# Encoder trunk on one core: the expert choice, ranks and slot lists made tile by tile inside the output projection, with four buffers of gathered rows

## Chip, cores and metric

One core of a Trainium2 chip runs the whole kernel in one launch. The metric is the device time of one execution in microseconds (us); lower is better.

## Reference

The reference is a trunk of two layers over 512 tokens of 1024 features, in float32. Layer 0 mixes tokens by windowed attention, layer 1 by a bidirectional gated DeltaNet. Both end with an output projection added to x, a row norm, and the same mixture of experts, cut here to what matters:

```python
def hierarchical_moe(h, w_group, b_group, w_expert, b_expert, w_gate, w_up, w_down):
    g_logits = t @ w_group + b_group                       # 4 groups
    g_prob, g_idx = lax.top_k(softmax(g_logits), 1)        # the best group
    e_sel = (t @ w_expert + b_expert).reshape(-1, 4, 8)[g_idx]
    e_prob, e_idx = lax.top_k(softmax(e_sel), 2)           # two of its 8 experts
    gate = g_prob * e_prob / sum(e_prob)
    hid = silu(t @ w_gate[e]) * (t @ w_up[e])              # 32 experts, 1024 -> 256
    return sum over the two experts of gate * (hid @ w_down[e])
```

## The kernel before

Tokens lie in four tiles (TT) of 128 rows. The order of the work is written out by hand for each engine, and semaphores join the engines. No planner is involved.

**Output projection** (`project_back_pe`, line 313). Two halves of 512 output columns, four tiles in each. One block is eight steps c of three matmuls (`three`, lines 142 to 144). In the second half each finished tile goes through a chain: VectorE adds the block to x (370), ScalarE squares the rows (249), VectorE and GpSimd make the root (263, 254), VectorE writes the normed rows hn (266), GpSimd stores them to h_rows in HBM (825), TensorE turns them (276), ScalarE and VectorE copy the two halves of the turned rows (288, 302), and TensorE multiplies them with the router (`route_pe`, 353: eight matmuls of 36 columns). VectorE adds the bias (359). `turn_routed` and `route_pe` for one tile stand behind the projection block of a later tile. The text calls the second half's block of tile t "block t"; route and turn of tile t are "route t" and "turn t".

**Choice and lists.** When all four tiles have logits, `moe_dve` (line 1046) works on all four at once: three times the first maximum (`first_max`: best group, best expert, second expert), one-hot rows `oh`, and their sum `oh_sum` (1074). TensorE counts with triangular and all-ones matrices (931 to 938) the rank of each token in its expert. VectorE picks the ranks (1084, 1086), compares them with slot numbers (1090), and eight matmuls of line 942 make the list of tokens of each expert. VectorE turns that into indices `idx_i` (1096).

**Experts.** GpSimd gathers the 64 slots of an expert from h_rows by an indirect DMA (`gather`, 833) into one of AHEAD = 8 row buffers, and scatters results to y_rows (`scatter`, 840). Its loop is

```python
for e in range(AHEAD):
    gather(e)
for e in range(EXPERTS):
    scatter(e)                      # waits y_copied of e
    if e + AHEAD < EXPERTS:
        gather(e + AHEAD)
```

TensorE runs for each expert e: gate and up (957), turn of the rows of e+1 (949), down of e-1 (966), turn of the hidden rows (999). VectorE copies the result of down (1119).

**Weights.** SyncE loads them in order (`moe_sync`, 2082): two of 1 MB for gate and up (2068) and one of 1 MB for down (2074) per expert. There are six homes for gate and up and five for down. Experts 1 and 2 may load when the first half of the projection is done, 3 when the second is, 4 when route 3 is (its home is ht), 5 when the normed rows are stored (its home is hn). From expert 6 on, gate and up wait until TensorE has used the home, and down of expert 5 waits for down of expert 0.

Of the kernel before, what the change touches and what calls it, by code (L numbers as in the profile page):

```python
# [10 lines left out]
AX = mybir.AxisListType.X  # L11

P = 128
D = 1024
# [25 lines left out]
AHEAD = 8  # L40
# [4 lines left out]
def build(nc, ap, out):  # L45
    ctx = ExitStack()
    with ctx:
# [265 lines left out]
        def project_back_pe(pe, k, n, tpk):  # L313
            for half in range(2):
                for t in range(TT):
# [383 lines left out]
        def masks_dve(dve, o):  # L699
# [15 lines left out]
            for l in range(1, LEVELS):  # L715
# [12 lines left out]
        at_xgt = ml.at  # L728
        xgt = ml.take(RING, KC * SLOTS)
        gated = ml.take(F // 2)  # L730
        at_hidden = ml.at
        hidden = ml.take(RING, F // 2)
        hidden_t = ml.take(RING, 2 * SLOTS)
        at_y = ml.at
# [34 lines left out]
        PER = dict(most=1, stored=16 * TT, routed=TT, logits=TT, pool_c=1, dve=2, exp_g=1, exp_e=1, onehots=1,  # L769
                   ranks=1, pos=1, placed=2 * TT, lists=1, idx=1, combined=TT)  # L770
# [156 lines left out]
        def moe_pe(pe, l):  # L927
            pe.wait_ge(s["onehots"], 1 + l * PER["onehots"])

            pe.matmul(bank[1][:, 0:TT * EXPERTS], upper[:, :], oh_sum.rearrange("p t e -> p (t e)"),  # L930
                      start=True, stop=False)
            for k in range(TT - 1):
                pe.matmul(bank[1][:, (k + 1) * EXPERTS:TT * EXPERTS].rearrange("p (t e) -> p t e", e=EXPERTS),
                          ones[:, :], oh_sum[:, k:k + 1, :].to_broadcast([P, TT - 1 - k, EXPERTS]),
                          start=False, stop=k == TT - 2)
            for k in range(TT):
                last = pe.matmul(bank[1][:, TT * EXPERTS:(TT + 1) * EXPERTS], ones[:, :], oh_sum[:, k, :],
                                 start=k == 0, stop=k == TT - 1)
            last.then_inc(s["ranks"], 1)
            for n in range(2 * TT):  # L940
                pe.wait_ge(s["placed"], n + 1 + l * PER["placed"])
                last = pe.matmul(bank[2][:, 0:2 * EXPERTS], at_slot[:, n // TT, n % TT, :],
                                 entries[:, n // TT, n % TT, :], start=n == 0, stop=n == 2 * TT - 1)
            last.then_inc(s["lists"], 1)

# [99 lines left out]

        def moe_dve(dve, l, o):
            lg = logits[:, :, 0:GROUPS]

# [3 lines left out]
            def first_max(src, n, col, dst):  # L1052

                o.step(dve.tensor_reduce(stat[:, col, :], src, AX, ALU.max))
                kk = key[:, :, 0:n]
                o.step(dve.tensor_tensor(kk, src, bc(stat[:, col, :], n), ALU.is_equal))
                o.step(dve.tensor_tensor(kk, kk, revs[:, 0:n].unsqueeze(1).to_broadcast([P, TT, n]), ALU.mult))
                o.step(dve.tensor_reduce(stat[:, 15, :], kk, AX, ALU.max))
                o.step(dve.tensor_tensor(dst, kk, bc(stat[:, 15, :], n), ALU.is_equal))

            dve.wait_ge(s["pool_c"], 1 + l * PER["pool_c"])
            dve.wait_ge(s["logits"], TT * (l + 1))
            first_max(lg, GROUPS, 0, oh_g)
            dve.tensor_tensor(g_exp, lg, bc(stat[:, 0, :], GROUPS), ALU.subtract).then_inc(s["dve"], 1)
            o.step(dve.tensor_scalar(oh_g, oh_g, -1.0, -REPEL, ALU.add, ALU.mult))
            e4 = "p t (g e) -> p t g e"
            o.step(dve.tensor_tensor(masked[:, 0].rearrange(e4, g=GROUPS),
                                     logits[:, :, GROUPS:].rearrange(e4, g=GROUPS),
                                     oh_g.unsqueeze(3).to_broadcast([P, TT, GROUPS, PER_GROUP]), ALU.add))
# [1242 lines left out]
```

## Time and profile before

| | |
|---|---|
| median of three runs | 1407.58 us (1407.0 to 1412.06) |
| the profiled execution, its own time | 1407.08 us |
| its span, first to last instruction | 1405.5 us |
| TensorE busy | 1223.2 us, 87% |
| VectorE / ScalarE / GpSimd busy | 584.0 / 384.5 / 464.5 us |
| mean granted TensorE clock | 0.945 |
| DMA | 270.29 MB, mean 192 GB/s |

The profile is one execution. "Busy" is the sum of the instructions of an engine. A float32 matmul shows as two records. The chain of waits follows the last instruction back to what released it; "issue" in it is time with nothing to see behind it. A window gives busy time, granted clock and the mean busy share of the 16 DMA engines. "To landing" is the time from the issue of a DMA to its completion.

### The profile page before, as it was taken

How to read it: one execution, taken by the hardware profiler on the slowest of the kernel's cores; microseconds unless marked ns; L12 is line 12 of the kernel's file. 1: busy time of each engine (PE TensorE's matmuls, PEld its weight loads, DVE VectorE, ACT ScalarE, POOL GpSimd, SP SyncE). 2: the span in 40 equal slices, each digit the busy share in tenths (PEclk: the TensorE clock that was granted, in tenths of full speed). 3: DMA queues.
4: the chain of work that ended last, by engine and by line, in shares of the span. 5: the costliest groups of instructions: out<-in, count | busy, mean ns of one | idle time of the engine just before them, and what ended most of it. 6: DMA issues, size and time to landing. Idle time of an engine off the chain costs nothing. (4 is left out here: it accounts for less than half of the span.)

```text
span 1405.5 us, 19363 instructions
## 1 busy us (share of the span) xinstructions
PE 1223.2 (87%) x7621; PEld 903.8 (64%) x7621; DVE 584.0 (42%) x1197; ACT 384.5 (27%) x804; POOL 464.5 (33%) x468
## 2 busy tenths in 40 slices
PE   5989999879998885889788999888999789998783
PEld 4867677755555552778677887678888755544451
DVE  4456754421111114564686455776464421111113
ACT  4325651111100012363433354433442211110000
POOL 1221001122222211046778247877221132222110
PEclk9999999879999998899999999999999889999997
DMA  7122004669999997211000111000235679999996
GB/s 219 61 66 76 1 1 187 249 255 374 382 388 388 385 409 316 80 60 60 2 0 1 60 61 60 1 0 2 97 113 211 267 282 377 395 386 378 386 417 238
DMA packets 65803, 270.29 MB, mean 192 GB/s; under 512 B 16812, under 2 KB 16908, under 8 KB 41136
## 3 DMA queue, kind: packets, MB, share of 16 engines
q1 hardware_dynamic: 54176, 247.50, 46.3%
q0 software_dynamic: 11392, 21.00, 4.5%
q8 instruction: 63, 1.03, 0.3%
q10 hardware_dynamic: 144, 0.52, 0.1%
q14 instruction: 28, 0.23, 0.1%
HBM read 262.69 MB, written 23.07 MB: 203 GB/s over the span
## 5 line engine op out<-in xcount | busy, mean ns | idle before, releaser
L840 POOL DMA_INDIRECT y_rows<-arena,idx_i x64 | 64.4, 1006 | 370.8 <-DVE arena L1119 362.6
L1455 PE MATMUL bank<-arena 128*128 128x128 f32 x1088 | 141.3, 287 | 16.8 <-DVE arena L1974 7.4
L1455 PEld LDWEIGHTS bank<-arena 128*128 128x128 f32 x1088 | 132.2, 199 | 29.4 <-DVE arena L1974 11.6
L957 PE MATMUL bank<-ring,arena 128*64 128x256 f32 x1024 | 127.8, 402 | 20.8 <-issue 19.8
L1123 DVE TENSOR_TENSOR arena<-arena,bank 128x128 f32<-128x128 f32 x64 | 18.4, 288 | 287.7 <-ACT arena L1034 287.7
L1034 ACT ACTIVATE arena<-bank 128x128 f32<-128x128 f32 x64 | 17.8, 277 | 388.3 <-PE bank L957 388.3
L957 PEld LDWEIGHTS bank<-ring,arena 128*64 128x64 f32 x1024 | 78.2, 139 | 60.0 <-issue 24.2
L144 PE MATMUL bank<-ring_r,ht_r 128*128 128x512 f32 x288 | 114.0, 396 | 0.0
L1119 DVE COPY arena<-bank 128x512 f32<-128x512 f32 x64 | 44.3, 692 | 144.4 <-PE bank L966 144.4
L142 PE MATMUL bank<-ring_r,arena_r 128*128 128x512 f32 (+1 forms) x228 | 92.2, 404 | 6.3 <-DVE ring_r L166 3.4
L143 PE MATMUL bank<-ring_r,arena_r 128*128 128x512 f32 x224 | 89.0, 398 | 0.0
L949 PEld LDWEIGHTS bank<-ident,arena 64*128 64x128 f32 x512 | 61.3, 200 | 34.9 <-issue 25.1
L143 PE MATMUL bank<-ht_r,ring_r 128*128 128x512 f32 (+1 forms) x224 | 82.0, 366 | 0.0
L833 POOL DMA_INDIRECT arena<-h_rows,idx_i x64 | 60.9, 952 | 61.6 <-DVE idx_i L1096 42.7
L949 PE MATMUL bank<-ident,arena 64*128 64x64 f32 x512 | 70.1, 278 | 9.4 <-DMA arena<-h_rows,idx_i 9.4
L1859 DVE SCALAR_TENSOR_TENSOR arena<-bank,arena 128x511 f32<-128x511 f32 (+1 forms) x72 | 54.0, 750 | 52.2 <-ACT arena L1572 50.5
L966 PE MATMUL bank<-ring,arena 128*64 128x512 f32 x304 | 73.6, 605 | 1.5 <-DVE arena L1128 1.5
L1782 POOL TENSOR_TENSOR arena<-ring,arena 128x512 f32<-128x512 f32 x48 | 61.9, 1309 | 6.9 <-PE bank L1455 6.9
L1757 POOL TENSOR_SCALAR arena<-arena,move 128x512 f32<-128x512 f32 x40 | 63.0, 1585 | 2.1 <-PE bank L1460 2.1
L144 PEld LDWEIGHTS bank<-ring_r,ht_r 128*128 128x128 f32 x288 | 55.2, 192 | 11.9
L276 PE MATMUL bank<-ident,hn 128*128 128x128 f32 x192 | 31.7, 320 | 33.3 <-DVE hn L266 31.5
L142 PE MATMUL bank<-ring_r 128*128 128x512 f32 (+1 forms) x144 | 56.8, 395 | 4.2 <-DVE ht_r L296 2.2
(297 smaller groups left out, 2373.7 us busy)
## 6 DMA issues: line engine op xcount, KB each, us to landing
ring<-in_moe_w_down SPq DMA_DIRECT2D x38, 1024.0 KB, 27.8
ring<-in_moe_w_gate SPq DMA_DIRECT2D x32, 1024.0 KB, 25.3
ring<-in_moe_w_up SPq DMA_DIRECT2D x32, 1024.0 KB, 27.8
ring<-in_gdn_w_in SPq DMA_DIRECT2D x8, 2048.0 KB, 8.2
arena<-in_moe_w_down SPq DMA_DIRECT2D x14, 1024.0 KB, 28.2
arena<-in_moe_w_gate SPq DMA_DIRECT2D x12, 1024.0 KB, 24.7
arena<-in_moe_w_up SPq DMA_DIRECT2D x12, 1024.0 KB, 26.6
gain<-in_moe_w_down SPq DMA_DIRECT2D x12, 1024.0 KB, 28.4
```

Source lines behind the costliest of these rows:

```text
L142: pe.matmul(dst, a[0], b[0], start=start, stop=False)
L143: pe.matmul(dst, a[0], b[1], start=False, stop=False)
L144: return pe.matmul(dst, a[1], b[0], start=False, stop=stop)
L833: pool.indirect_dma_start(out=rows_of(e), out_offset=None, in_=h_rows[l], in_offset=bass.IndirectOffsetOnAxis(ap=idx_i[0:SLOTS, 0, e:e + 1 ...
L840: pool.indirect_dma_start(out=y_rows[l], out_offset=bass.IndirectOffsetOnAxis(ap=idx_i[:, 1, e:e + 1], axis=0), in_=y_out[:, e % RING, :], ...
L949: last = pe.transpose(bank[0][:, c * SLOTS:(c + 1) * SLOTS], rows_of(e)[:, c::KC], ident[at, at])
L957: last = pe.matmul(bank[1][m * SLOTS:(m + 1) * SLOTS, 0:2 * P].rearrange("p (w n) -> p w n", w=2), xgt[:, i, c * SLOTS:(c + 1) * SLOTS], w ...
L966: last = pe.matmul(bank[3][half * SLOTS:(half + 1) * SLOTS, :], hidden_t[:, i, m * SLOTS:(m + 1) * SLOTS], d[:, m, half * HALF:(half + 1) ...
L1455: last = pe.matmul(bank[b][:, h * P:(h + 1) * P], lhs(h), rhs(h), start=True, stop=True)
L1757: pool.tensor_scalar(s_buf[slot], r_buf[l % 2][slot], move[:, l:l + 1], None, ALU.mult).then_inc(g["rb"], 1)
L1782: pool.tensor_tensor(lm[slot], lt_of(n), by_head(level[l]), ALU.mult).then_inc(g["lm"], 1)
L1859: last = dve.scalar_tensor_tensor(out=acc, in0=bank[U % 4][:, of], scalar=tap(k, unit), in1=acc, op0=ALU.mult, op1=ALU.add)
```

## The change

The choice moves from `moe_dve` into the projection. VectorE runs route_dve and `choose_dve` of tile 0 ahead of its wait for block 2, and of tile 1 ahead of block 3; tiles 2 and 3 follow behind the projection. Route 0 and route 1 on TensorE stand now inside blocks 2 and 3, behind their step c = 1. Ranks are made per tile from a running sum (`oh_upto`), lists per tile, and the totals last, behind the list. Scratch of the choice moves to where row buffers 4 to 7 were, so AHEAD is 4: four gathers are issued ahead, and gather e+4 stands behind scatter e. `first_max` has four operations on one tile where it had five on all four.

```diff
 RING = 3
-AHEAD = 8
+AHEAD = 4
...
                             split_done(pe, n + half, c)
                         last = three(pe, bank[u % 4][:, :], ht_parts(tpk, c, slice(t * P, (t + 1) * P)),
                                      panel_parts(n + half, c, slice(0, PANEL)), c == 0, c == KC - 1)
+                        if half and t >= 2 and c == 1:
+                            route_pe(pe, k, tpk + 1, t - 2)
                     last.then_inc(back, 1)
                     if k and u == 0:
                         pe.wait_ge(g["ready"], TT)
@@ -330,12 +332,42 @@
                     if half and t:
                         pe.wait_ge(ln["rows"], TT * (2 * k + 1) + t)
                         turn_routed(pe, k, tpk + 1, t - 1)
-                    if half and t >= 2:
-                        route_pe(pe, k, tpk + 1, t - 2)
             route_pe(pe, k, tpk + 1, TT - 2)
             pe.wait_ge(ln["rows"], TT * (2 * k + 1) + TT)
             turn_routed(pe, k, tpk + 1, TT - 1)
+            for t in range(2):
+                ranks_pe(pe, k, t)
             route_pe(pe, k, tpk + 1, TT - 1)
+            ranks_pe(pe, k, 2)
+            for t in range(2):
+                lists_pe(pe, k, t)
+            ranks_pe(pe, k, 3)
+            for t in range(2, TT):
+                lists_pe(pe, k, t)
+
+        def rank_bank(t):
+            return bank[(1, 1, 3, 0)[t]][:, t * EXPERTS:(t + 1) * EXPERTS]
+
+        def ranks_pe(pe, l, t):
+            if t == 0:
+                pe.wait_ge(x_half, 2 * TT * l + 2 * TT)
+            pe.wait_ge(s["onehots"], TT * l + t + 1)
+            at = rank_bank(t)
+            last = pe.matmul(at, upper[:, :], oh_sum[:, t, :], start=True, stop=t == 0)
+            if t:
+                last = pe.matmul(at, ones[:, :], oh_upto[:, t - 1, :], start=False, stop=True)
+            last.then_inc(s["ranks"], 1)
+
+        def lists_pe(pe, l, t):
+            for k in range(2):
+                pe.wait_ge(s["placed"], 2 * TT * l + 2 * t + k + 1)
+                last = pe.matmul(bank[2][:, 0:2 * EXPERTS], at_slot[:, k, t, :], entries[:, k, t, :],
+                                 start=t + k == 0, stop=t + k == TT)
+            if t == TT - 1:
+                last.then_inc(s["lists"], 1)
+                pe.wait_ge(s["totals"], l + 1)
+                pe.matmul(bank[3][:, 0:EXPERTS], ones[:, :], oh_upto[:, TT - 1, :], start=True, stop=True
+                          ).then_inc(s["counted"], 1)
 
         def turn_routed(pe, l, k, t):
...
 
         x_half = sem("x_half")
 
-        def project_back_dve(dve, k, tpk):
+        def project_back_dve(dve, k, tpk, o):
             for half in range(2):
                 for t in range(TT):
                     u = TT * half + t
+                    if half and t >= 2:
+                        route_dve(dve, k, t - 2)
+                        choose_dve(dve, k, t - 2, o)
                     dve.wait_ge(back, 2 * TT * k + u + 1)
                     dst = x[:, t, half * PANEL:(half + 1) * PANEL]
                     dve.tensor_tensor(dst, dst, bank[u % 4][:, :], ALU.add).then_inc(x_half, 1)
@@ -372,11 +407,14 @@
                         if t:
                             turn_dve(dve, tpk + 1, t - 1)
                         norm_dve(dve, 2 * k + 1, t)
-                        if t >= 2:
-                            route_dve(dve, k, t - 2)
             route_dve(dve, k, TT - 2)
+            groups_dve(dve, k, TT - 2, o)
             turn_dve(dve, tpk + 1, TT - 1)
+            experts_dve(dve, k, TT - 2, o)
+            for t in range(2):
+                place_dve(dve, k, t, o)
             route_dve(dve, k, TT - 1)
+            choose_dve(dve, k, TT - 1, o)
 
         def project_back_act(act, k, tpk):
...
-        at_slot = cut(at_xgt, 2, TT, P)
-        entries = cut(at_y, 2, TT, 2 * EXPERTS)
-        key = cut(at_hidden, TT, EXPERTS)
-        oh_sum = cut(at_hidden + TT * EXPERTS, TT, EXPERTS)
-        masked = cut(at_hidden + 2 * TT * EXPERTS, 2, TT, EXPERTS)
+        rl = Layout()
+        rl.at = AHEAD // 2 * D
+        at_slot = rl.take(2, TT, P)
+        at_entries = rl.at
+        entries = rl.take(2, TT, 2 * EXPERTS)
+        key = rl.take(EXPERTS)
+        masked = rl.take(2, EXPERTS)
+        placed_in = rl.take(2, EXPERTS)
+        oh_sum = rl.take(TT, EXPERTS)
+        oh_upto = rl.take(TT, EXPERTS)
+        assert rl.at <= 2 * D * 2
+        pos_parts = cut(at_entries, 2, TT, EXPERTS)
...
         def moe_pe(pe, l):
-            pe.wait_ge(s["onehots"], 1 + l * PER["onehots"])
...
-            last.then_inc(s["lists"], 1)
...
 
+        def first_max(dve, o, src, n, t, col, dst, op, scale):
+
+            o.step(dve.tensor_reduce(stat[:, col, t:t + 1], src, AX, ALU.max))
+            kk = key[:, 0:n]
+            o.step(dve.scalar_tensor_tensor(out=kk, in0=src, scalar=stat[:, col, t:t + 1], in1=revs[:, 0:n],
+                                            op0=ALU.is_equal, op1=ALU.mult))
+            o.step(dve.tensor_reduce(stat[:, 15, t:t + 1], kk, AX, ALU.max))
+            o.step(dve.tensor_scalar(dst, kk, stat[:, 15, t:t + 1], scale, op, ALU.mult))
+
+        def groups_dve(dve, l, t, o):
+            if t == 0:
+                dve.wait_ge(s["pool_c"], 1 + l * PER["pool_c"])
+            dve.wait_ge(s["logits"], TT * l + t + 1)
+            first_max(dve, o, logits[:, t, 0:GROUPS], GROUPS, t, 0, oh_g[:, t, :], ALU.is_lt, REPEL)
+            e4 = "p (g e) -> p g e"
+            o.step(dve.tensor_tensor(masked[:, 0].rearrange(e4, g=GROUPS), logits[:, t, GROUPS:].rearrange(e4, g=GROUPS),
+                                     oh_g[:, t, :].unsqueeze(2).to_broadcast([P, GROUPS, PER_GROUP]), ALU.add))
+
+        def experts_dve(dve, l, t, o):
+            first_max(dve, o, masked[:, 0], EXPERTS, t, 1, oh[:, 0, t, :], ALU.is_equal, 1.0)
+            o.step(dve.scalar_tensor_tensor(out=masked[:, 1], in0=oh[:, 0, t, :], scalar=2 * REPEL, in1=masked[:, 0],
+                                            op0=ALU.mult, op1=ALU.add))
+            first_max(dve, o, masked[:, 1], EXPERTS, t, 2, oh[:, 1, t, :], ALU.is_equal, 1.0)
+            last = dve.tensor_tensor(oh_sum[:, t, :], oh[:, 0, t, :], oh[:, 1, t, :], ALU.add)
+            if t < TT - 1:
+                o.step(last)
+                last = dve.tensor_scalar(oh_upto[:, t, :], oh_sum[:, t, :], 0.0, None, ALU.add) if t == 0 else                     dve.tensor_tensor(oh_upto[:, t, :], oh_upto[:, t - 1, :], oh_sum[:, t, :], ALU.add)
+            last.then_inc(s["onehots"], 1)
+            for k in range(2):
+                dve.tensor_tensor(entries[:, k, t].rearrange("p (w e) -> p w e", w=2),
+                                  oh[:, k, t].unsqueeze(1).to_broadcast([P, 2, EXPERTS]),
+                                  listed[:, k, :, t].unsqueeze(2).to_broadcast([P, 2, EXPERTS]), ALU.mult)
+
+        def choose_dve(dve, l, t, o):
+            groups_dve(dve, l, t, o)
+            experts_dve(dve, l, t, o)
+
+        def place_dve(dve, l, t, o):
+            dve.wait_ge(s["ranks"], TT * l + max(t + 1, 2))
+            found = rank_bank(t)
+            o.step(dve.tensor_tensor(placed_in, oh[:, :, t, :], found.unsqueeze(1).to_broadcast([P, 2, EXPERTS]),
+                                     ALU.mult))
+            o.step(dve.tensor_reduce(rank_f[:, :, t], placed_in, AX, ALU.add))
+            for k in range(2):
+                dve.tensor_scalar(at_slot[:, k, t, :], slot_no, rank_f[:, k, t:t + 1], None, ALU.is_equal
+                                  ).then_inc(s["placed"], 1)
+
         def moe_dve(dve, l, o):
...
+            dve.tensor_tensor(g_exp, logits[:, :, 0:GROUPS], bc(stat[:, 0, :], GROUPS), ALU.subtract
+                              ).then_inc(s["dve"], 1)
             dve.tensor_tensor(stat[:, 5, :], stat[:, 2, :], stat[:, 1, :], ALU.subtract).then_inc(s["dve"], 1)
...
+            for t in range(2, TT):
+                place_dve(dve, l, t, o)
+            dve.wait_ge(s["onehots"], TT * (l + 1))
+            dve.tensor_tensor(oh_upto[:, TT - 1, :], oh_upto[:, TT - 2, :], oh_sum[:, TT - 1, :], ALU.add
+                              ).then_inc(s["totals"], 1)
             dve.wait_ge(s["lists"], 1 + l * PER["lists"])
             for w in range(2):
                 last = dve.tensor_scalar(idx_i[:, w, :], bank[2][:, w * EXPERTS:(w + 1) * EXPERTS],
                                          first_of[:, w:w + 1], None, ALU.add)
             last.then_inc(s["idx"], 1)
+            dve.wait_ge(s["counted"], 1 + l * PER["counted"])
+            o.step(dve.tensor_reduce(most_f, bank[3][:, 0:EXPERTS], AX, ALU.max))
+            dve.tensor_copy(most_i[:, :], most_f).then_inc(s["most"], 1)
             for k in range(2):
-                last = dve.tensor_tensor(masked[:, k], oh[:, k], base.unsqueeze(1).to_broadcast([P, TT, EXPERTS]),
...
```

## Rows read from the trace of the kernel before

**Rows 1.** Windows of layer 1: length, busy us (instructions) by engine, clock, DMA share, GB/s.

```profile
1130.00:1135.00 5.00, 1.37 (x10) 1.22 (x12) 0.90 (x6) 0.94 (x2) 3.78 (x5) 0.50 0.52 153
1210.00:1220.00 10.00, 10.00 (x72) 5.21 (x70) 2.06 (x5) 0.86 (x2) 2.41 (x3) 1.00 1.03 395
1260.00:1270.00 10.00, 7.32 (x52) 4.29 (x50) 1.40 (x4) 0.86 (x2) 1.96 (x2) 1.00 1.02 361
```

**Rows 2.** Chain of waits, layer 1, late experts: start, us, what.

```profile
1260.33 2.67 issue
```

**Rows 3.** Timeline, layer 1, second half of the projection: start us, us, engine, line.

```profile
1090.43 0.48 PE L142 MATMUL bank<-ring_r,arena_r 128*128 128x512 f32 x1
...
1104.14 1.04 PE L276 MATMUL bank<-ident,hn 128*128 128x128 f32 x8
...
1104.34 0.69 DVE L370 TENSOR_TENSOR x<-x,bank 128x512 f32<-128x512 f32 x1 [4.01 <-PE bank L144]
...
1105.01 3.69 PE L353 MATMUL bank<-router,ht 128*128 128x36 f32 x32
...
1106.11 0.56 ACT L288 COPY ht<-bank 128x512 f32<-128x512 f32 x1
...
1107.07 1.28 DVE L266 SCALAR_TENSOR_TENSOR hn<-x,norm_s,gain 128x1024 f32<-128x1024 f32 x1 [0.68 <-POOL norm_s L254]
...
1110.57 3.28 PE L353 MATMUL bank<-router,ht 128*128 128x36 f32 x16 [0.88 <-DVE ht L302]
```

**Rows 4.** Timeline, layer 1, choice, lists, first gather and turn.

```profile
1114.19 0.17 DVE L1054 TENSOR_REDUCE arena<-arena 128x4 f32<-128x16 f32 x1
...
1114.39 0.18 DVE L1056 TENSOR_TENSOR arena<-arena 128x16 f32<-128x16 f32 x1
...
1119.41 0.29 DVE L1074 TENSOR_TENSOR arena<-arena 128x128 f32<-128x128 f32 x1
...
1121.48 1.89 PE L937 MATMUL bank<-arena,ones 128*128 128x32 f32 x8
...
1124.39 1.66 DVE L1090 TENSOR_SCALAR arena<-arena 128x128 f32<-128x128 f32 x8
...
1124.74 3.68 PE L942 MATMUL bank<-arena 128*128 128x64 f32 x16 [1.36 <-DVE arena L1090]
...
1129.74 1.04 POOL L833 DMA_INDIRECT arena<-h_rows,idx_i  x1 [20.52 <-DVE idx_i L1096]
...
1132.81 1.14 PE L949 MATMUL bank<-ident,arena 64*128 64x64 f32 x8 [4.39 <-DMA arena<-h_rows,idx_i]
```

**Rows 5.** Timeline, layer 1, loop over experts: turns of 3 and 4, gather of 5.

```profile
1152.70 1.09 PE L949 MATMUL bank<-ident,arena 64*128 64x64 f32 x8
...
1158.53 0.95 POOL L833 DMA_INDIRECT arena<-h_rows,idx_i  x1 [0.30 <-issue]
...
1159.63 1.09 PE L949 MATMUL bank<-ident,arena 64*128 64x64 f32 x8
```

**Rows 6.** Timeline, layer 0: last add, first gather and turn.

```profile
264.19 0.69 DVE L370 TENSOR_TENSOR x<-x,bank 128x512 f32<-128x512 f32 x1 [4.02 <-PE bank L144]
...
291.26 1.04 POOL L833 DMA_INDIRECT arena<-h_rows,idx_i  x1 [22.17 <-DVE idx_i L1096]
...
294.89 1.15 PE L949 MATMUL bank<-ident,arena 64*128 64x64 f32 x8 [5.01 <-DMA arena<-h_rows,idx_i]
```

**Rows 7.** DMA issues between 1116 and 1118 us: KB, us to landing.

```profile
gain<-in_moe_w_down SPq DMA_DIRECT2D x1, 1024.0 KB, 15.0
```

**Rows 8.** DMA issues between 1129.5 and 1130 us, the first gather.

```profile
arena<-h_rows,idx_i POOLq DMA_INDIRECT x1, 3.0
```

**Rows 9.** DMA issues between 1151 and 1152 us, the gather of expert 4.

```profile
arena<-h_rows,idx_i POOLq DMA_INDIRECT x1, 6.9
```

**Rows 10.** All gathers: us to landing.

```profile
DMA to landing us min/median/max: 2.8/7.6/8.9
```

**Rows 11.** DMA queues of the whole span: packets, MB, share of 16 engines.

```profile
q0 software_dynamic: 11392, 21.00, 4.5%
```

More of the change, by code:

```diff
@@ L768, in build @@
         late_step = [sem(f"late_step{l}") for l in range(2)]
-        PER = dict(most=1, stored=16 * TT, routed=TT, logits=TT, pool_c=1, dve=2, exp_g=1, exp_e=1, onehots=1,
-                   ranks=1, pos=1, placed=2 * TT, lists=1, idx=1, combined=TT)
+        PER = dict(most=1, totals=1, counted=1, stored=16 * TT, routed=TT, logits=TT, pool_c=1, dve=2, exp_g=1, exp_e=1, onehots=TT,
+                   ranks=TT, pos=1, placed=2 * TT, lists=1, idx=1, combined=TT)
         PER.update({n: EXPERTS for n in ("st", "turned", "xgt", "up", "silu", "hidden", "hid_turned", "hid_t",
@@ L927, in moe_pe @@
         def moe_pe(pe, l):
-            pe.wait_ge(s["onehots"], 1 + l * PER["onehots"])
[L930 to L943, printed above, removed]
-            last.then_inc(s["lists"], 1)
             def turn_rows(e):
@@ L1046, in moe_dve @@
         def moe_dve(dve, l, o):
-            lg = logits[:, :, 0:GROUPS]
             def bc(v, n):
                 return v.unsqueeze(2).to_broadcast([P, TT, n])
[L1052 to L1069, printed above, removed]
@@ L1070, in moe_dve @@
-            first_max(masked[:, 0], EXPERTS, 1, oh[:, 0])
-            o.step(dve.scalar_tensor_tensor(out=masked[:, 1], in0=oh[:, 0], scalar=2 * REPEL, in1=masked[:, 0],
-                                            op0=ALU.mult, op1=ALU.add))
-            first_max(masked[:, 1], EXPERTS, 2, oh[:, 1])
-            dve.tensor_tensor(oh_sum, oh[:, 0], oh[:, 1], ALU.add).then_inc(s["onehots"], 1)
-            dve.tensor_tensor(stat[:, 5, :], stat[:, 2, :], stat[:, 1, :], ALU.subtract).then_inc(s["dve"], 1)
@@ L1076, in moe_dve @@
-            for k in range(2):
-                dve.tensor_tensor(entries[:, k].rearrange("p t (w e) -> p t w e", w=2),
-                                  oh[:, k].unsqueeze(2).to_broadcast([P, TT, 2, EXPERTS]),
-                                  listed[:, k].rearrange("p w t -> p t w").unsqueeze(3).to_broadcast(
-                                      [P, TT, 2, EXPERTS]), ALU.mult)
-            dve.wait_ge(s["ranks"], 1 + l * PER["ranks"])
-            found = bank[1][:, 0:TT * EXPERTS].rearrange("p (t n) -> p t n", t=TT)
@@ L1083, in moe_dve @@
-            for k in range(2):
-                last = dve.tensor_tensor(masked[:, k], found, oh[:, k], ALU.mult)
-            o.step(last)
-            o.step(dve.tensor_reduce(rank_f.rearrange("p k t -> p (k t)"), masked.rearrange("p k t e -> p (k t) e"),
-                                     AX, ALU.add))
-            for k in range(2):
-                for t in range(TT):
-                    dve.tensor_scalar(at_slot[:, k, t, :], slot_no, rank_f[:, k, t:t + 1], None, ALU.is_equal
-                                      ).then_inc(s["placed"], 1)
@@ L1098, in moe_dve @@
             last.then_inc(s["idx"], 1)
+            dve.wait_ge(s["counted"], 1 + l * PER["counted"])
+            o.step(dve.tensor_reduce(most_f, bank[3][:, 0:EXPERTS], AX, ALU.max))
+            dve.tensor_copy(most_i[:, :], most_f).then_inc(s["most"], 1)
             for k in range(2):
-                last = dve.tensor_tensor(masked[:, k], oh[:, k], base.unsqueeze(1).to_broadcast([P, TT, EXPERTS]),
+                last = dve.tensor_tensor(pos_parts[:, k], oh[:, k], base.unsqueeze(1).to_broadcast([P, TT, EXPERTS]),
                                          ALU.mult)
             o.step(last)
-            o.step(dve.tensor_reduce(pos_f.rearrange("p k t -> p (k t)"), masked.rearrange("p k t e -> p (k t) e"),
-                                     AX, ALU.add))
+            o.step(dve.tensor_reduce(pos_f.rearrange("p k t -> p (k t)"),
+                                     pos_parts.rearrange("p k t e -> p (k t) e"), AX, ALU.add))
             o.step(dve.tensor_tensor(pos_f, pos_f, rank_f, ALU.add))
@@ L2288, in _ @@
             gdn_dve(dve, o)
-            project_back_dve(dve, 1, 4)
+            project_back_dve(dve, 1, 4, o)
             moe_dve(dve, 1, o)
```

8 lines of the change are left out of this document (2 added, 6 removed).

## The prediction

> **What bounds the kernel now.** I read the windows first, then the chain of waits, the timeline around the end of the projection, and last the DMA issues. From 1210 us on, a window of layer 1 has the DMA engines at a share of 1.03 and 395 GB/s while TensorE is fully busy; from 1260 us the share is still 1.02, but TensorE is busy for 7.32 of 10 us [rows 1], and the chain shows why: 2.67 us of "issue" ahead of a gate and up, which is a wait for weights [rows 2]. An expert needs 3 x 1024 KB = 3.15 MB, at 395 GB/s 7.96 us. TensorE needs only 1159.63 - 1152.70 = 6.93 us for an expert [rows 5]. So the stage of the experts is bound by the weight stream, after TensorE has first run through what was prefetched. The one hole in the stream is at its start: at 1130 to 1135 us the DMA share is 0.52 [rows 1], because all homes are full and nothing is freed until the first experts are done. The end of each layer therefore stands at a fixed distance behind the moment when expert 0 is turned and multiplied, and this moment is what the change can shift. Two layers, two shifts; everything behind a layer moves along with it.
>
> From the last add of x (E, 1104.34) to the first gather is 25.4 us in layer 1 [rows 3, 4], 27.1 us in layer 0 (264.19 to 291.26) [rows 6]. This stretch holds small work in single file, and is what the change shortens.
>
> **1. Inside blocks 2 and 3.** From the start of block 2 to E are 13.9 us [rows 3], and they contain two blocks, one turn and route 0. Now they contain route 1 too. 16 route records at full clock are 3.69/2 = 1.85 us [rows 3]. At step c = 1 TensorE has to wait for the copies of the turned tile: the ScalarE copy ends 1106.11 + 0.56 - 1104.34 = 2.33 us behind an add [rows 3], which itself starts some 0.1 behind the block, against 2.3 us of turn and six matmuls. With a wake-up that is about 0.2 us a block, taken as 0.35 for both. E moves by **+2.2 us**. VectorE's choice of a tile lies beside this. It has five operations for the group, nine for the experts, two for the sums, two for the entries: 18. Small operations follow each other by 1114.39 - 1114.19 = 0.20 us [rows 4], with 32 columns I take 0.22, so 3.9 us. It can start when the route inside the block ends, and 18 matmuls at 0.23 us (5.5 us for a block's 24) are 4.1 us more of the block. It just fits; if this cover is gone, each us too many delays the add behind it, and at tile 3 E itself.
>
> The Trainium skill, page "VectorE: DVE Perf Modes", section "The TRN2 errata — SBUF-src ops pay a fixed extra latency per instruction", speaks against this part: many small tiles pay a fixed cost per tile that one large one pays once. The trace agrees: 0.17 us for 16 columns, 0.29 us for 128 [rows 4], so four tiles cost 15.6 us of choice, where all four together took 5.5 us from 1114.19 to the end of the sum [rows 4]. By the rule VectorE's sum rises, and the time only if the cover fails.
>
> **2. Behind E.** In us from the new E. Route 2 can't start before the copy, at 2.35; before, route 1 covered this wait. At full clock it ends at 4.2. Normed rows of tile 3 are there at 1107.07 + 1.28 - 1104.34 = 4.0 [rows 3]. Turn 3 takes 1.04 at full clock [rows 3]. By then the granted clock falls from 1.00 to 0.50 (2.4 to 1.2 GHz): it is 0.50 at 1130 us [rows 1], and route 3 took 3.28 for 16 records where 3.69 was the time of 32 [rows 3], a ratio of 1.8. So I take 1.8 for turn 3, to 6.0; VectorE's copy to 6.7. Then VectorE has the experts of tile 2 (11 steps and two entries, 2.7, the groups having run before the copy) to 9.4, and two places. A place is two steps and two comparisons of 1.66/8 = 0.21 [rows 4], together 0.9: to 11.2. TensorE meanwhile makes ranks 0 and 1, six records at 1.89/8 = 0.24 [rows 4], to 7.4, and route 3 at the lower clock to 10.7. So VectorE is late now, not TensorE. Choice 3 up to the one-hots is 16 steps, 3.5: 14.7. Entries and two small operations 0.55, place 2 0.9, place 3 0.8: 17.0. The last list matmuls, 0.23 a record (3.68/16) [rows 4], 0.5: 17.5. From the last list matmul (1128.42) to the gather stay 1.3 us, indices and GpSimd's wake [rows 4]. The gather is issued at **18.8**, where it was 25.4. Less the 2.2 of step 1, the gain is 4.4 us in layer 1. In layer 0 the same stretch was 1.7 us longer, from an earlier fall of the clock; I give the new one 0.7 of it: 27.1 - 19.5 - 2.2 = 5.4 us. Together **-9.8 us**. The bounds: if the clock fell nowhere, about 1 us a layer better, since VectorE's chain remains; if small operations follow each other by 0.30 in place of 0.22, some 33 of them behind E cost 2.6 us a layer more, and the choices inside the blocks up to 1.4 (18 x 0.08).
>
> The totals matmul and the positions come behind the indices; their cover is the first gather, the turn and gate and up of expert 0, and VectorE has nothing else to do until then. Norm, store and root keep their order on GpSimd. Its only queue change is that four gathers in place of eight stand ahead of scatter 0, which waits for expert 0 anyway. Two memsets fewer per layer lie far ahead of any need.
>
> **3. The first gather meets the weight stream.** This gives most back. The weights of experts 3 to 5 are freed by the end of the projection, by route 3 and by the stored rows. The last of them was issued between 1116 and 1118 us and landed 15.0 us later, at some 1132.6 [rows 7]; the stream was thinning at 1130 to 1135 [rows 1]. The first gather, at 1129.74, landed in 3.0 us [rows 4, 8]; in layer 0, 3.6 us passed to the turn [rows 6]. Now the stream is freed later: route 3 ends at E + 10.7 + 2.2, before it ended at 1113.85, so 3.4 us later in layer 1; I take 2 in layer 0, where its route 3 was late already. And the gather comes 4.4 and 5.4 us earlier. It is thus in the middle of a full stream. Gathers in a full stream take 6.9 us [rows 9] and up to 8.9, in the median 7.6 [rows 10]. Bounds: 3.0 and 8.9. I take 6.9, the row that had the least in front of it, as the nearest to a gather with no scatter ahead. Landing costs +3.9 and +3.3, together **+7.2 us**.
>
> The Trainium skill, page "DMA: Bandwidth & Descriptors", section "Queues, rings and completion order", says that a DMA engine takes turns between its queues, a packet at a time. Read as an equal turn, the gather would hardly be held, and the sum would be that of the first rival below. The rows speak of 4 us more in a full stream [rows 8, 9].
>
> **4. Four gathers move into the bound stretch.** Gathers 4 to 7 ran in the hole of the stream. Now they stand behind scatters 0 to 3, in the full stream. The software queue moved 21.00 MB [rows 11]; without eight stores of 512 KB, 16.8 MB in 128 gathers and scatters, 0.13 MB each. Four are 0.53 MB, at 395 GB/s 1.3 us a layer: **+2.7 us**. It costs nothing if the hole was filled otherwise.
>
> **5. Four buffers in the loop.** Gather e+4 stands behind scatter e. From turn 3 to the issue of gather 5, which is where it will stand too, are 1158.53 - 1152.70 = 5.83 us [rows 5]. Turn e+4 can't come before turn e+2 plus 5.83 plus the landing L, so an expert takes at least (5.83 + L)/2: 6.7 us at 7.6, 7.4 at 8.9 [rows 10]. Both are under the 7.96 us of the weights. TensorE will show short waits for rows early in the stage; these cost nothing, as the stream stays full. Cost 0.
>
> **Sum.** -9.8 + 7.2 + 2.7 = +0.1 us on the profiled execution's 1407.08 (span 1405.5 and 1.6 around it), half a us under the median of 1407.58. Forecast **1407 us**, no change. A measurement of this kernel can tell about 0.5% from no change, 7 us: 1400.5 to 1414.6.
>
> **Rivals.**
>
> *The gather isn't held by the stream.* It lands in 3.0 and 3.6 us as now; term 3 falls away, and the time is 1407.1 - 9.8 + 2.7 = 1400.0. For it: two rings side by side, and a landing of 3.0 us when the stream was only just thinning. Against: 6.9 us at 1151, and 7.6 in the median of all [rows 9, 10]. Chance 0.18; with term 4 at zero too it would be 1397.
>
> *Rows come too late with four buffers (slower).* The place is the turn of e+4. It decides from (5.83 + L)/2 = 7.96, so L = 10.1 us. At L = 11 an expert takes 8.4 us, 0.45 over the stream, for some 27 experts a layer: +24 us, 1431. For it: 8.9 was seen, and gathers are now never early. Against: none of 64 was over 8.9, and contention in the loop is the same. Chance 0.07.
>
> *The choice doesn't fit beside the blocks.* If an operation follows by 0.35 us, the choice takes 6.3 us, and adds, normed rows and all behind are later by 2.2 us a tile; the chain behind E grows by 3.5. Then the gather comes as late as before or later, with the DMA queue emptier: about +3 us a layer and +2.7, 1416. Against: the 0.20 us seen. Chance 0.06.
>
> *It does not do what it says*: the start of the first expert is set by the end of the stream alone, not by the gather. This would again be 1407 to 1411. It is part of the forecast's case.
>
> **How the numbers follow.** The forecast's case (the gather in the stream, 5 to 9 us) has 0.60 and spans 1403 to 1412. 0.09 is left for terms that move both ways within 0.5%. Faster by over 0.5% is 0.18 and a little of the forecast's tail, 0.20. Slower by over 0.5% is 0.13. Same is 0.67. The range has to reach over the first rival at 1400.0, and takes in 8.9 us of landing in both layers (2.0 us more than mine in each, 1411) and a late choice in part: 1399 to 1414.
>
> **What the profile after would show.** Right: E 2.2 us later relative to the start of block 2; VectorE at work at the ends of blocks 2 and 3; the first gather about 25.4 - 4.4 = 21 us behind the old place of E; its landing near 7 us, where it was 3.0; the first turn within 1 us of its old place; short waits of TensorE for gathered rows from expert 5 on, and less "issue" late in the stage. Wrong: a first gather that lands in 3 to 4 us; adds of x that wait for VectorE rather than for TensorE; a DMA share under 1 in the middle of the stage, or an expert that takes over 8 us while weights lie ready.

## The result, and the profile after

| | before | changed |
|---|---|---|
| median | 1407.29 us (6 runs) | 1418.01 us (6 runs) |
| lowest and highest | 1403.39, 1412.06 | 1414.75, 1421.65 |
| profiled execution / its span | 1407.08 / 1405.5 | 1414.75 / 1413.1 |
| VectorE busy | 584.0 us | 602.6 us |
| mean granted TensorE clock | 0.945 | 0.942 |

The ratio is 1.0076, 95% interval 1.0058 to 1.0094: slower by 10.7 us, where 1407 and a range up to 1414 were forecast.

I read the after profile at the same places. Windows of layer 1 (length, busy us by engine, clock, DMA share, GB/s):

```profile
1130.00:1135.00 5.00, 1.14 (x8) 0.95 (x8) 0.00 (x0) 0.40 (x1) 0.51 (x1) 0.50 1.05 311
1210.00:1220.00 10.00, 10.00 (x79) 5.68 (x77) 1.65 (x5) 0.86 (x2) 3.64 (x4) 1.00 1.02 360
1260.00:1270.00 10.00, 9.00 (x69) 5.32 (x65) 1.18 (x3) 0.86 (x2) 3.65 (x4) 1.00 1.02 388
```

The share in the full stream is as before [rows 1]: the stage of the experts is still bound by the weights. But at 1130 us the stream is still full (1.05 in place of 0.52). The rates of the two later windows tell nothing by themselves: at 1210 us it is 360 GB/s in place of 395, at 1260 us 388 in place of 361.

The timeline of layer 1, from the add of tile 1, the last that nothing of the change has touched, to the first turn:

```profile
1088.24 0.69 DVE L405 TENSOR_TENSOR x<-x,bank 128x512 f32<-128x512 f32 x1 [1.36 <-PE bank L144]
...
1105.54 0.68 DVE L405 TENSOR_TENSOR x<-x,bank 128x512 f32<-128x512 f32 x1
...
1107.93 2.42 PE L385 MATMUL bank<-router,ht 128*128 128x36 f32 x16 [1.56 <-ACT ht L288]
...
1110.15 1.95 PE L276 MATMUL bank<-ident,hn 128*128 128x128 f32 x8
...
1117.66 0.16 DVE L1073 TENSOR_REDUCE arena<-arena 128x1 f32<-128x4 f32 x1
...
1121.04 0.19 DVE L1094 TENSOR_TENSOR arena<-arena 128x32 f32<-128x32 f32 x1
...
1125.77 1.04 POOL L876 DMA_INDIRECT arena<-h_rows,idx_i  x1 [15.34 <-DVE idx_i L1132]
...
1133.37 1.14 PE L974 MATMUL bank<-ident,arena 64*128 64x64 f32 x8 [8.55 <-DMA arena<-h_rows,idx_i]
```

The same add in the kernel before:

```profile
1089.83 0.69 DVE L370 TENSOR_TENSOR x<-x,bank 128x512 f32<-128x512 f32 x1 [1.36 <-PE bank L144]
```

From this add to the last one are 1105.54 - 1088.24 = 17.30 us, before 1104.34 - 1089.83 = 14.51 [rows 3]. The last add has no idle time of VectorE before it. The last matmul of block 3 tells whether the choice held it, after and before:

```profile
1105.10 0.40 PE L144 MATMUL bank<-ring_r,ht_r 128*128 128x512 f32 x1
...
1103.90 0.40 PE L144 MATMUL bank<-ring_r,ht_r 128*128 128x512 f32 x1
```

The add starts 0.44 us behind its start in both (before at 1104.34), so TensorE set it. Choice 3 takes from 1117.66 to 1121.04 up to the sum, for all of the tile. The first gather goes out at 1125.77, 20.2 us behind the last add, before 25.4 [rows 3, 4]. Its rows are turned 7.60 us later, before 3.07 [rows 4].

Layer 0, block 2 and the tail:

```profile
248.78 1.95 PE L385 MATMUL bank<-router,ht 128*128 128x36 f32 x16 [0.20 <-issue]
...
250.77 0.20 DVE L391 TENSOR_TENSOR arena<-bank,router_b 128x36 f32<-128x36 f32 x1 [0.39 <-PE bank L385]
...
254.76 0.35 DVE L1100 TENSOR_TENSOR arena<-arena 128x64 f32<-128x64 f32 x2
...
255.03 0.68 DVE L405 TENSOR_TENSOR x<-x,bank 128x512 f32<-128x512 f32 x1
...
263.64 0.68 DVE L405 TENSOR_TENSOR x<-x,bank 128x512 f32<-128x512 f32 x1
...
283.01 1.05 POOL L876 DMA_INDIRECT arena<-h_rows,idx_i  x1 [14.48 <-DVE idx_i L1132]
...
291.07 1.14 PE L974 MATMUL bank<-ident,arena 64*128 64x64 f32 x8 [9.05 <-DMA arena<-h_rows,idx_i]
```

Choice 0 takes from 250.77 to 255.11, 4.3 us with the bias. The gather comes 19.4 us behind the last add, before 27.1 [rows 6], and the turn 8.06 us behind the gather, before 3.63.

The chain of waits of layer 1 shows the landing of the gather of expert 4 (issued at 1152.74, there 9.31 us later) and, late in the stage, still waits for weights:

```profile
1152.74 9.31 DMA arena<-h_rows,idx_i
...
1372.95 1.57 issue
```

To place the loss I split each layer by five marks of the timeline: the add of tile 1, the last add, the first gather, the first turn, the first copy of a down result, the last scatter. All are differences of start times in the one profiled execution of each kernel.

| us | before, layer 0 / 1 | changed, layer 0 / 1 | change |
|---|---|---|---|
| add of tile 1 to last add | 14.51 / 14.51 | 17.30 / 17.30 | +2.8 / +2.8 |
| to the first gather | 27.07 / 25.40 | 19.37 / 20.23 | -7.7 / -5.2 |
| to the first turn | 3.63 / 3.07 | 8.06 / 7.60 | +4.4 / +4.5 |
| to the first copy of down | 16.76 / 15.98 | 16.18 / 16.55 | -0.6 / +0.6 |
| to the last scatter | 237.25 / 236.31 | 240.83 / 242.88 | +3.6 / +6.6 |
| sum | | | +2.5 / +9.3 |

Each layer's column adds up to the last line; together that is +11.8 us. The stretches outside, which the change doesn't touch, came out 4.1 us shorter in this execution, so that the spans differ by 7.6; the medians, 10.7. The first four lines nearly cancel, at +1.7 us. The surprise is the last, the loop over the experts. Where in the loop it lies is seen in the copies of down of experts 0, 24 and 31 in layer 1. Before:

```profile
1148.79 0.69 DVE L1119 COPY arena<-bank 128x512 f32<-128x512 f32 x1 [2.31 <-PE bank L966]
...
1333.40 0.69 DVE L1119 COPY arena<-bank 128x512 f32<-128x512 f32 x1 [2.30 <-PE bank L966]
...
1383.64 0.69 DVE L1119 COPY arena<-bank 128x512 f32<-128x512 f32 x1 [2.08 <-PE bank L966]
```

After:

```profile
1149.92 0.69 DVE L1158 COPY arena<-bank 128x512 f32<-128x512 f32 x1 [2.31 <-PE bank L991]
...
1335.76 0.69 DVE L1158 COPY arena<-bank 128x512 f32<-128x512 f32 x1 [2.31 <-PE bank L991]
...
1391.33 0.69 DVE L1158 COPY arena<-bank 128x512 f32<-128x512 f32 x1 [2.08 <-PE bank L991]
```

Expert 0 to 24: 184.6 and 185.8 us. Expert 24 to 31: 50.2 and 55.6 us (layer 0: 184.0 and 185.4, then 51.8 and 54.0). Most of the loss is at the end of the stage. Before, experts 24 to 31 ran with hardly a gather beside them, since gather e+8 is issued behind scatter e. Now gathers 28 to 31 stand there. TensorE waits for rows early in the loop (58.7 and 59.7 us from expert 0 to 8 in the two layers, before 55.4), but in neither layer behind expert 16.

The trace before held the price already. Gate and up of experts 19, 24 and 31 in layer 1:

```profile
1272.23 3.84 PE L957 MATMUL bank<-ring,arena 128*64 128x256 f32 x32 [2.25 <-issue]
...
1318.00 3.85 PE L957 MATMUL bank<-arena 128*64 128x256 f32 x32 [0.67 <-issue]
...
1375.07 3.85 PE L957 MATMUL bank<-ring,arena 128*64 128x256 f32 x32 [0.94 <-issue]
```

Experts 19 to 24 start 9.15 us apart, experts 24 to 31 8.15. Windows of the same trace, the first with weights alone, the second with gathers and scatters, the third with a scatter and no gather:

```profile
1126.00:1129.00 3.00, 2.41 (x12) 2.22 (x11) 0.85 (x7) 0.00 (x0) 0.00 (x0) 0.50 1.00 423
1179.00:1187.00 8.00, 8.00 (x61) 4.40 (x59) 1.18 (x3) 0.86 (x2) 2.73 (x4) 1.00 1.02 377
1345.00:1352.00 7.00, 6.12 (x45) 3.50 (x42) 1.18 (x3) 0.86 (x2) 0.29 (x1) 1.00 1.00 418
```

With gathers the rate is a tenth lower at the same busy share, so the share alone doesn't show what the stream loses.

### The profile page after: what moved, and what is told of

Its sections match the earlier page's. It is cut to its first block and busy times, and to the rows that moved or that the text cites. A ratio compares the mean times of both kernels' runs of the same rounds, so it can differ in the third digit from the quotient of the medians.

```text
span 1413.1 us, 19475 instructions
## 1 busy us (share of the span) xinstructions
PE 1224.1 (87%) x7621; PEld 898.7 (64%) x7621; DVE 602.6 (43%) x1309; ACT 384.4 (27%) x804; POOL 463.1 (33%) x464
## 3 DMA queue, kind: packets, MB, share of 16 engines
q8 instruction: 63, 1.03, 0.3%
## 5 line engine op out<-in xcount | busy, mean ns | idle before, releaser
L1494 PE MATMUL bank<-arena 128*128 128x128 f32 x1088 | 138.4, 283 | 17.7 <-DVE arena L2013 8.4
L1494 PEld LDWEIGHTS bank<-arena 128*128 128x128 f32 x1088 | 129.1, 195 | 30.5 <-DVE arena L2013 12.0
```

The costliest lines, as they stand in the source:

```text
L1494: last = pe.matmul(bank[b][:, h * P:(h + 1) * P], lhs(h), rhs(h), start=True, stop=True)
```

## The experiments

My theory T was **traffic**: a gather beside the full stream takes some 1 us from it, not the 0.33 us of its bytes. The rivals are L, **lateness** (TensorE waits for rows with four buffers); C, **collision** (the first gather lands late because it stands in the weight stream), which I took as a second loss; and the theory that the loss is in the new route and choice themselves.

### e1: the kernel before with four buffers

```diff
-AHEAD = 8
+AHEAD = 4
...
         xg = ml.take(AHEAD // 2, D)
+        ml.at = 4 * D
```

> The kernel before with four row buffers in place of eight and nothing else changed (gathers 4 to 7 move behind scatters 0 to 3). Theory T, traffic: in the trace before, experts 19 to 24 of layer 1, which run beside a gather each, start 9.15 us apart, and experts 24 to 31, beside none, 8.15 us; so a gather takes about 1 us from the weight stream, and four moved ones cost 4 us a layer: +8 us, 1415. Theory L, lateness: TensorE waits for rows in experts 4 to 9 (some 0.4 us each); this would give +4 to +8 too, but with a loss that is already there at expert 16. The recorded forecast priced the move at 1.3 us a layer: +2.7 us, 1410.

Measured 1418.57 us, ratio 1.0076 (1.0053 to 1.0099), as much as the whole loss of the change. Its copies of down of experts 0, 24 and 31 in layer 1:

```profile
1156.02 0.69 DVE L1120 COPY arena<-bank 128x512 f32<-128x512 f32 x1 [2.31 <-PE bank L967]
...
1341.69 0.69 DVE L1120 COPY arena<-bank 128x512 f32<-128x512 f32 x1 [2.30 <-PE bank L967]
...
1397.90 0.69 DVE L1120 COPY arena<-bank 128x512 f32<-128x512 f32 x1 [2.08 <-PE bank L967]
```

Expert 0 to 24 is 185.7 us, 24 to 31 is 56.2 (layer 0: 183.7 and 56.1, before 184.0 and 51.8). Up to expert 8 it had lost 3 us to late rows (58.5 from expert 0 to 8, before 55.4). Layer 0 has made them up at expert 16 (114.9, before 114.7); in layer 1 they are still there at 16 (114.3, before 111.3), and 1.1 us of them at 24. Lateness is there, as forecast, and costs little; how little, e4 shows. The recorded 2.7 us for the move is refuted: the interval starts at 7.5 us.

### e2: the changed kernel with eight buffers

```diff
-AHEAD = 4
+AHEAD = 8
...
-        rl.at = AHEAD // 2 * D
+        rl.at = 2 * D
...
             dve.tensor_copy(pos_i[:, :, :], pos_f).then_inc(s["pos"], 1)
+            for i in (2, 3):
+                dve.memset(xg[:, i, :], 0.0).then_inc(s["pos"], 1)
...
             def gather(e):
+                if e == 4 or e == 6:
+                    pool.wait_ge(s["pos"], e // 2 + l * PER["pos"])
```

GpSimd clears only the first four buffers, and two semaphores of the totals become further counts of others.

> The changed kernel with eight row buffers; the scratch of the choice stays where it is and VectorE clears buffers 4 to 7 behind the positions, before gathers 4 to 7 go out. Theories T and L: both losses go, 8 us under the changed kernel, about 1410. If the loss of the change is in its route and choice and not in the buffers: 1418, no change.

Measured 1409.94 us, ratio 1.0017 (1.0000 to 1.0034). The loop is back to 237.1 and 235.6 us from the first copy to the last scatter. So the new order of route, choice, ranks and lists alone gains nothing; it stands 2.8 us on the slow side. What it saves in series, the landing of the first gather gives back.

### e3: the weights of expert 5 held until the first turn

```diff
         kept_rows = [(s["stored"], 16 * TT * (l + 1)), (tp["turned"], 2 * TT * (TPN[2 * l + 1] + 1)),
+                     (s["turned"], 1 + l * PER["turned"])]
```

> The changed kernel with one wait more on the weight queue: the loads of expert 5 (and all behind) go out when the rows of expert 0 have been turned. Theory C, collision: the first gather, which took 8.0 and 7.6 us to the turn in the middle of the stream, meets an almost empty stream and lands in 3.0 to 4 us; the first turn is 4 us earlier in each layer, the weights of expert 5 still fit in the hole: -8 us, 1410. Rival: the landing is slow for another reason (writes of the rows of tile 3, the first use of the queue): then 0 or, with the weights later, up to +2 us.

Measured 1411.25 us, ratio 1.0026 (1.0012 to 1.0040), 6.8 us under the changed kernel. First gather, first turn, and the held loads in layer 1:

```profile
1126.65 1.04 POOL L876 DMA_INDIRECT arena<-h_rows,idx_i  x1 [15.36 <-DVE idx_i L1132]
...
1129.59 1.14 PE L974 MATMUL bank<-ident,arena 64*128 64x64 f32 x8 [3.90 <-DMA arena<-h_rows,idx_i]
...
1130.81 0.33 SPq L2107 DMA_DIRECT2D hn<-in_moe_w_gate  x1
```

2.94 us from gather to turn, in layer 0 3.66. The windows from gather to turn in layer 1, with the hold and in the changed kernel:

```profile
1126.65:1129.60 2.95, 0.01 (x1) 0.02 (x1) 1.40 (x8) 0.00 (x0) 2.34 (x3) 0.50 0.18 51
...
1125.77:1133.40 7.63, 0.03 (x1) 0.04 (x1) 1.40 (x8) 0.00 (x0) 3.83 (x4) 0.50 1.03 381
```

Theory C holds: the 7.6 to 8.1 us from gather to turn come of the weight stream.

### e4: gather ahead of scatter, four buffers

```diff
             for e in range(EXPERTS):
-                scatter(e)
                 if e + AHEAD < EXPERTS:
                     gather(e + AHEAD)
+                scatter(e)
```

> The changed kernel with the loop turned around: gather e+4 is issued before scatter e, so it waits only for the turn of e, about one expert earlier. Bytes are the same. Theory T: only gather 4 moves into the hole of the stream, -1 us a layer, -2 us, 1416. Theory L: the waits of TensorE for rows are gone, and with them the whole loss of the experts' stage, -6 to -8 us, 1411.

Measured 1416.42 us, ratio 1.0067 (1.0045 to 1.0089). In its trace TensorE doesn't wait for rows behind the first turn (55.4 us from expert 0 to 8 in both layers, as before), and yet experts 0 to 31 take 239.1 and 238.3 us, in the changed kernel 239.4 and 241.4. The 6 to 8 us of theory L are not there. The 1.6 us are what one gather a layer in the hole would give, but they are within the scatter of the medians.

### e5: without the last four gathers

The last four experts of a layer work on the rows that lie in their buffers; the count of landings per layer (`rows_in`) is made to fit.

```diff
...
-                if e + AHEAD < EXPERTS:
+                if e + AHEAD < EXPERTS - 4:
                     gather(e + AHEAD)
...
-                pe.wait_ge(xg_full[e % AHEAD], rows_in(l, e))
+                if e < EXPERTS - 4:
+                    pe.wait_ge(xg_full[e % AHEAD], rows_in(l, e))
```

> The changed kernel without gathers 28 to 31 of each layer: these four experts work on the rows that lie in their buffers, so their results are other ones; nothing else is left out. 24 gathers stand behind scatters, as in the kernel before. Theory T (each gather in the bound stretch takes 1.0 to 1.5 us from the weights): experts 24 to 31 take 50 to 52 us as before, not 54 to 56, and the time falls by 8 to 12 us, to 1407 to 1410. Theory L (lateness of rows in the early experts): 1418, no change. By bytes alone (1.3 us a layer): 1415.

Measured 1411.85 us, ratio 1.0026 (1.0007 to 1.0045): 6.2 us less for eight gathers, 0.8 each, under the 8 to 12 I expected. In its trace the loops are 10.7 us shorter than in the changed kernel, 1.3 each. Experts 24 to 31 took 50.7 and 50.8 us, as before.

### e6 and e9: 24 gathers a layer issued twice, with rows and without

```diff
                 if e + AHEAD < EXPERTS:
                     gather(e + AHEAD)
+                if 4 <= e < 28:
+                    n = 24 * l + e - 4
+                    if n >= 2:
+                        pool.wait_ge(again[n % 2], 16 * (n // 2))
+                    at = SLOTS * (e % 2)
+                    pool.indirect_dma_start(
+                        out=spare[at:at + SLOTS, 0, :], out_offset=None, in_=h_rows[l],
+                        in_offset=bass.IndirectOffsetOnAxis(ap=idx_i[0:SLOTS, 0, e:e + 1], axis=0),
+                        bounds_check=SEQ - 1, oob_is_err=False).then_inc(again[n % 2], 16)
```

In e9 the indices are `idx_no`, all 60000, out of bounds.

> The changed kernel with 24 gathers a layer (experts 4 to 27) issued a second time, into spare memory that nobody reads, behind the gather of the loop. Theory T: 24 x 1.0 to 1.5 us in each layer, +48 to +72 us, 1466 to 1490. By bytes alone, 0.33 us each: +16 us, 1434.

> As e6, but the 24 second gathers a layer have only indices out of bounds, so they move no rows; all else (instruction, queue, semaphore) is the same. If the 1.2 us of a gather (57.7 us for 48 in e6) are a fixed cost of the instruction and its descriptors: 1475. If they are a cost of moving its rows beside the weights: near the changed kernel's 1418, at most 1425.

e6: 1475.73 us, 57.7 over the changed kernel, 1.20 us for each of 48. Copies of down of experts 0, 24, 31 in its layer 0:

```profile
307.54 0.69 DVE L1168 COPY arena<-bank 128x512 f32<-128x512 f32 x1 [2.31 <-PE bank L1001]
...
510.85 0.69 DVE L1168 COPY arena<-bank 128x512 f32<-128x512 f32 x1 [2.30 <-PE bank L1001]
...
573.33 0.69 DVE L1168 COPY arena<-bank 128x512 f32<-128x512 f32 x1 [2.08 <-PE bank L1001]
```

265.8 us from 0 to 31, in the changed kernel 239.4: 26.4 for 24 gathers, 1.10 each (layer 1: 28.5, 1.19 each). e9: 1425.91 us, 7.9 over, 0.16 each; in its trace the loops grew by 1.9 us in all, 0.04 each, and the rest stands outside them. So the price lies in moving the rows beside the weights, not in the instruction or its queue. Each of the two has only two measured executions.

### e7: eight buffers and the hold

e2 and e3 together.

> The changed kernel with eight row buffers (as in e2) and the loads of expert 5 held until the first turn (as in e3). If the two losses are separate they add up: 1418 - 8 - 7 = 1403, 4 us under the kernel before. If the hold only shifts what the hole of the stream takes up: 1407 to 1410.

Measured 1406.45 us, ratio 1.0002 (0.9987 to 1.0017). The gains add up only in part: the first turn comes 3.52 and 2.84 us behind the gather, but the loop takes 239.5 us in both layers against 237.1 and 235.6 in e2. In both, experts 24 to 31 run as before; the loss stands earlier (expert 0 to 24 is 189 us in both layers, in e2 183.5 and 185.3), where the held 3 MB and gathers 1 to 7 fill the hole. That this is the reason was not tested by a run of its own.

### e8: the slots spread over the partitions

```diff
-            pool.iota(slot_no.rearrange("p (h j) -> p h j", h=2), [[0, 2], [1, SLOTS]], base=0,
+            pool.iota(slot_no.rearrange("p (h a b) -> p h a b", h=2, a=16), [[0, 2], [1, 16], [16, 4]], base=0,
```

> The kernel before with the slots of an expert spread over the partitions: partition p of a half holds slot 16 (p mod 4) + p div 4, in place of slot p. Some 32 of 64 slots are filled, from 0 up, so the filled rows lie now in all of the 64 partitions and not in the lower half. Theory S: a gather costs four times its bytes because its rows lie in a few partitions and are moved by a part of the 16 DMA engines, while the weights wait for the slowest; spread, gathers and scatters cost the stream less: 5 to 30 us under 1407. If rows are dealt to the engines in another way: 1407, no change.

Measured 1409.58 us, ratio 1.0018 (1.0001 to 1.0034). Theory S falls. The windows above show that the engines move less at the same share while rows run beside; why they do is open.

### e10, e11, e12: gathers into the hole

e10 is the edit of e4 on the kernel before, e11 on e7.

> The kernel before, eight row buffers, with the loop turned around: gather e+8 ahead of scatter e. Gathers 8 and 9, perhaps 10, are then issued behind turns 0, 1 and 2, before the first down projection, in the hole of the stream, and 21 or 22 stand in the bound stretch in place of 24. Theory T (1.2 us each): 2 to 3 of them a layer, -5 to -7 us, 1400 to 1402. Theory L, or no effect: 1406.

> The changed kernel with eight buffers, the hold of expert 5's loads (e7), and the loop turned around as in e10. If the hole has room beside the held weights: 5 us under e7, 1401. If the held weights fill the hole already, so that the gathers only change places with them: 1406, as e7.

e10: 1405.56 us, ratio 0.9982 (0.9964 to 0.9999). My expectation had a slip: scatter 0 holds the queue behind gather 8, so one gather a layer moves, which at 1.2 us is 2.4 of the 5 to 7; measured against the runs beside it, 1.8. e11: 1407.90 us, ratio 1.0000 (0.9987 to 1.0014), no better than e7; its hole was full, as the second of the two expectations has it. e12 corrects the slip:

```diff
-            for e in range(AHEAD):
+            for e in range(AHEAD + 2):
                 gather(e)
             for e in range(EXPERTS):
+                if e + AHEAD + 2 < EXPERTS:
+                    gather(e + AHEAD + 2)
                 scatter(e)
-                if e + AHEAD < EXPERTS:
-                    gather(e + AHEAD)
```

> The kernel before, eight row buffers, with gather e+10 ahead of scatter e: gathers 8, 9 and 10 are issued behind turns 0, 1 and 2 and ahead of scatter 0, so 21 gathers a layer stand in the bound stretch in place of 24. (In e10 only gather 8 had moved, since scatter 0 held the queue behind it.) Theory T at 1.2 us a gather: 3 x 1.2 x 2 = -7 us, 1400. Gather 10 is issued only 3 us before the stream is full again, so it may count in part: 1402. No effect of gathers: 1407.

Measured 1399.71 us, against 1405.82 beside it, ratio 0.9949 (0.9932 to 0.9966). It is the fastest of all kernels here, with neither the new choice nor four buffers. Copies of down of experts 0, 24, 31 in its layer 1:

```profile
1147.43 0.69 DVE L1119 COPY arena<-bank 128x512 f32<-128x512 f32 x1 [2.29 <-PE bank L966]
...
1328.03 0.69 DVE L1119 COPY arena<-bank 128x512 f32<-128x512 f32 x1 [2.31 <-PE bank L966]
...
1377.39 0.69 DVE L1119 COPY arena<-bank 128x512 f32<-128x512 f32 x1 [2.08 <-PE bank L966]
```

Expert 0 to 24 takes 180.6 us, before 184.6.

All traces together give the price once more. The table has the time from the first copy of down to the last scatter, both layers added, against the gathers behind scatter 0 in each layer.

| gathers a layer behind scatter 0 | both loops, us |
|---|---|
| 52 (e6) | 538.6 |
| 28 (changed, e1, e3) | 483.7, 484.6, 483.5 |
| 27 (e4) | 480.4 |
| 24 (before, e2, e5, e8) | 473.6, 472.7, 473.0, 474.0 |
| 23 (e10) | 470.0 |
| 21 (e12) | 463.8 |

These are 1.1 to 1.8 us a gather. e7 (24) and e11 (23), with eight buffers and the hold, stand apart at 479.0 and 480.6.

## Why the prediction was wrong

**What bounds the kernel** was right: the DMA share stays at 1.02 in both, the end hangs on the weight stream, and the shift of the first expert passes through.

**Step 1, E +2.2 us:** measured +2.8, all of it on TensorE: from the start of block 2 to the start of the last matmul of block 3 it took 16.27 us in layer 1, before 13.47. The route between the blocks had cost 1.8 us; each of the two inside a block cost 2.3, so the excess was 1.0 us for both, where 0.35 was put. The choice with its bias took 4.3 us, not 3.9 to 4.1, since steps with a per-partition operand take 0.22 to 0.25 us. The adds of tiles 2 and 3 start with no idle time of VectorE before them, but in layer 1 they come as soon behind the last matmul of their block as before (0.44 us at tile 3), or 0.1 us later (tile 2). The choice just fitted, as said, and that rival is out.

**Step 2, the chain behind E:** -6.6 and -7.6 us forecast, -5.2 and -7.7 measured. In layer 1 the lower clock came during route 2 (2.42 us for 16 records, 1.98 in layer 0), so the copy of turn 3 was 0.7 us late; by the end of choice 3 it was 1.0, at the gather 1.4. VectorE and not TensorE was late behind it, as said. That layer 0 came out so close is in part luck: over the traces this stretch takes 25.1 to 27.1 us in the old order and 19.4 to 21.1 in the new.

**Step 3, the first gather in the stream:** +3.9 and +3.3 forecast, +4.5 and +4.4 measured; e3 showed the cause. The first rival, a gather not held, at 1400, is out. The Trainium skill ("DMA: Bandwidth & Descriptors", "Queues, rings and completion order") says that a DMA engine takes turns between its queues, a packet at a time; that didn't save a small transfer from 4 to 5 us of delay here.

**Step 4 is the step that failed.** "Four are 0.53 MB, at 395 GB/s 1.3 us a layer: +2.7 us." The mechanism was right and the size was not. The loop grew by 3.6 and 6.6 us a layer; e1 gives 11.4 us for this step alone, e2 8.1, e6 1.2 us a gather with its row traffic (9.6 for eight), e5 0.8 (6.2 for eight). I divided bytes by the rate of the stream, as if a gather took from it no more than its own bytes. The rows for a better price were in the trace before: experts 24 to 31 start 8.15 us apart in layer 1, experts 19 to 24 9.15. The spread from 6.2 to 11.4 us is not explained; the medians scatter by some us, and some of e1's may be lateness.

**Step 5, four buffers in the loop cost 0 by lateness:** right within what can be told. The waits for rows are there (3.3 and 4.3 us up to expert 8, and the gather of 9.31 us in the chain at 1152.74). e4 took them away, and moved a gather into the hole as well, and the medians fell by 1.6 us in all. The slower rival had the right sign and the wrong mechanism.

By terms, the forecast of +0.1 missed the profiled pair's +11.8 us by 1.2 in step 1, 1.3 in step 2, 1.8 in step 3 and 7.4 in step 4. The first three alone would have left the time within the range.

## What to carry to other kernels

In a stage that a weight stream bounds, price a small gather by what the stream loses in the trace (spacing of loop turns with and without one), not by its bytes. Count how many small transfers stand in the stream and how many in its holes before buffers are given up for scratch: here four buffers more were worth 8 to 11 us (e2, e1), the serial work that their memory made room to hide 7.3 us (steps 1 and 2), of which the slower landing took back all; three gathers more in the hole gave 0.5% alone. Who shortens a chain that ends in a DMA must look at what else is on the DMA engines at the new time.

## What the runs showed of the hardware

A gather of 64 indices, with 0.13 MB of rows on average, takes 1.2 us from a stream of some 390 GB/s, more than three times its 0.33 us by bytes; the same instruction with no valid index takes 0.04 (loops of the trace) to 0.16 us (medians) (e6, e9). The DMA share stays at 1.00 to 1.02 while the rate is 423 GB/s with weights alone, 418 with a scatter and 377 with gathers and scatters. Spreading the valid rows over the partitions gave nothing (e8). From the issue of the first gather to its turn pass 2.8 to 3.9 us where the DMA share between them is 0.15 to 0.72 (before, e1, e3, e7, e8, e10, e11, e12), and 7.4 to 8.7 us where it is 1.01 to 1.03 (changed, e2, e4, e5, e6, e9).
